# A gated recurrence inside a long one-core program: decay levels on column quarters of TensorE, and the value units read out of PSUM by ScalarE

## The chip, the cores and the metric

The program runs on one core of one Trainium2 chip. The metric is the device time of one execution in microseconds (us). A core has TensorE (PE in the profile, with its weight loads on a row of their own, PEld), VectorE (DVE), ScalarE (ACT), GpSimd (POOL) and SyncE (SP). Each runs its own queue of instructions in order, and they meet through semaphores. Matmul results land in PSUM, eight banks of 128 x 512 fp32 values; everything else lives in SBUF.

## The reference, cut to what matters

The program computes four layers of a model (each a feed-forward net, a mixer, a second feed-forward net and a gate) and then a second block, on 256 tokens of width 1024. Layers 0 and 3 use the mixer that the change touches, a gated recurrence with 8 heads of 128 features and chunks of 64 tokens:

```
def hgrn2_mixer(x, lb, w_in, g_norm, w_out):
    q, f, i, og = jnp.split(x @ w_in, 4, axis=-1)
    q = jax.nn.silu(q)
    log_f = jnp.logaddexp(jnp.log(lb), jnp.log1p(-lb) + jax.nn.log_sigmoid(f))
    k = (1.0 - lb) * jax.nn.sigmoid(-f)
    ...
    def step(S, inp):
        q_, k_, v_, g_ = inp
        b = jnp.cumsum(g_, axis=2)
        o_inter = jnp.einsum('bhtk,bhkv->bhtv', q_ * jnp.exp(b), S)
        diff = b[:, :, :, None, :] - b[:, :, None, :, :]
        decay = jnp.exp(jnp.where(causal[:, :, None], diff, -jnp.inf))
        A = jnp.einsum('bhtk,bhsk,bhtsk->bhts', q_, k_, decay)
        o_intra = jnp.einsum('bhts,bhsv->bhtv', A, v_)
        ...
    o = rmsnorm(from_chunks(o), g_norm)
    o = o.reshape(B, T, D_MODEL).astype(x.dtype) * jax.nn.silu(og)
    return o @ w_out
```

The values v are the columns `i` of the projection, one factor of the input norm per token.

## The kernel before

**Projections.** All weights arrive as units of 128 x 2048 fp32 values (1 MB), 405 of them in the order of use. ACT rounds a unit to the fp32r format (`high`, L1153: `w_hi`), DVE subtracts that from the unit (`low`, L1559: `w_lo`), and PE multiplies in three passes (high by high, low by high, high by low), so a unit is 48 matmuls of 256 columns: `project` (L670) with the weights stationary, `project_tokens` (L687) with the tokens stationary. There are three slots of split units. `high(m)` waits until unit m-3 has been used, `low(m)` waits for `high(m)`, and the projection of unit m waits for `low(m)`. So the end of unit u on PE releases `high(u+3)` on ACT, and that releases `low(u+3)` on DVE.

**The mixer's stages.** Units 0 to 3 give the forget gate, 4 to 7 the queries, 8 to 11 the values, 12 to 15 the output gate, 16 to 19 the output projection. A value unit is projected into one of two PSUM banks with the tokens on the partitions. `tokens(u)` evicts it into `HG_V`: two 128 x 256 operations with one factor per token (`rcol`), on DVE by `scale_tokens` (L1624). The last of the two raises `bank_read`, which counts evicted banks.

**The levels.** The matrix of decayed scores A of each head and block of 128 tokens is built from a diagonal (`diagonal`, L799) and seven levels l = 0 to 6 with windows w = 1, 2, 4, 8, 16, 32 and 64: at level l, the queries of the upper half of every window of 2w tokens meet the keys of the lower half of the same window. `level(l)` on PE (L819) runs over 16 groups of 128 tokens in two halves of eight. In levels 0 to 5 a group is two fp32 matmuls, one for each block of 64 tokens: 64 keys stationary, 32 queries moving, the result on partitions 0 to 63 or 64 to 127 of PSUM. Level 6 is one matmul a group. Each fp32 matmul leaves two records in the trace, each with a weight load of its own.

Between the levels DVE multiplies the decays of one more window into the queries and keys (`grow(l)`, L1826 and L1827, twice each, for the two halves). `grow(l)` waits for `level(l)`, since it overwrites its operands, and half of `level(l+1)` waits for the same half of `grow(l)`. For the levels 0 to 3 DVE copies the results that a mask picks out of PSUM into `HG_AT` (`take(l)`, L1842). For 4 to 6 ACT copies rectangles (L1276). `across` (L830) comes after level 6 in the same way.

**Order of the work.** It is written by hand. PE: unit 8, diagonal, level 0, unit 9, level 1, first half of unit 10, level 2, rest of unit 10, a quarter of unit 11, level 3, rest of unit 11, level 4, half of unit 12, level 5, rest of unit 12, a quarter of unit 13, level 6. DVE: evict 8, low 11, grow 0, diagonal, take 0, evict 9, low 12, grow 1, take 1, grow 2, evict 10, low 13, take 2, grow 3, take 3, evict 11, low 14, grow 4, grow 5, evict 12, low 15, grow 6. ACT in this stage has the `high` of units 11 to 14 and then the rectangles. Units from 12 on are evicted by `scale` (L1618) on DVE.

Of the kernel before, what the change touches and what calls it, by code (L numbers as in the profile page):

```python
# [11 lines left out]
ACT = mybir.ActivationFunctionType  # L12
AX_X = mybir.AxisListType.X

P = 128
T = 256
TB = T // P
# [16 lines left out]
HD = 64  # L34
# [186 lines left out]


LEVELS = (1, 2, 4, 8, 16, 32, 64)
MASKED = 4
NEG = -1e30

# [81 lines left out]
def build(nc, phases, x_t, p_t, mem_t, weights, smalls_d, post_rows, c_common, c_levels, c_swa, c_second, out):  # L308
    begin = starts(phases)
    NU = begin[-1]["units"]  # L310
    with ExitStack() as ctx:
# [235 lines left out]
        def level_bank(l):  # L547

            return 2 + (4 + 2 * l) % 6

        def upper(v, w):

            return v.rearrange("p (n a w) -> p n a w", a=2, w=w)[:, :, 1, :]
# [94 lines left out]
        def _(pe):  # L648
# [137 lines left out]
            def hg(i):  # L786
                m = own[i]
                n0, e0 = at(i, "units"), at(i, "banks")
                mixer_head(i)
                for u in range(4, 8):  # L790
                    project(n0 + u, e0 + u, XG)

                def diagonal():
                    pe.wait_ge(bank_read, e0 + 8 + 4)
                    pe.wait_ge(m["forget"], 4)
                    pe.wait_ge(m["qsilu"], 4)
                    for g in range(16):
                        h, b = g // 2, g % 2
                        last = nc.tensor.matmul(ps[:, 2 + g // 4, (g % 4) * P:(g % 4 + 1) * P],  # L799
                                                HG_K[:, h, b * P:(b + 1) * P], HG_Q[:, h, b * P:(b + 1) * P],  # L800
                                                start=True, stop=True)
                    last.then_inc(m["diag"], 1)

                def level(l):
                    w = LEVELS[l]
                    if l in (1, 2):
                        pe.wait_ge(m["masked"], 1)
                    elif 3 <= l <= 6:
                        pe.wait_ge(m["masked"], l - 1)
                    for half in range(2):  # L810
                        pe.wait_ge(m["qk"], 2 * l + half + 1)
                        for g in range(8):
                            at_ = (8 * half + g) * P
                            queries = P if w == HD else HD
                            for t in range(P // queries):
                                own_half = slice(at_ + t * HD, at_ + t * HD + queries)
                                c = g * HD + t * queries // 2
                                o = ps[t * HD:(t + 1) * HD, level_bank(l) + half, c:c + queries // 2]
                                last = nc.tensor.matmul(o.rearrange("p (n w) -> p n w", w=w),  # L819
                                                        HG_SUFFIX[:, own_half.start:own_half.start + HD],  # L820
                                                        upper(HG_PQ[:, own_half], w), start=True, stop=True)
                        last.then_inc(m["level"], 1)

                def across():
                    l = len(LEVELS)
                    pe.wait_ge(m["copied"], 1)
                    for half in range(2):
                        pe.wait_ge(m["qk"], 2 * l + half + 1)
                        for h in range(4 * half, 4 * half + 4):
                            last = nc.tensor.matmul(ps[:, level_bank(l) + half, (h % 4) * P:(h % 4 + 1) * P],  # L830
                                                    HG_SUFFIX[:, h * T:h * T + P], HG_PQ[:, h * T + P:(h + 1) * T],
                                                    start=True, stop=True)
                        last.then_inc(m["level"], 1)

                def outputs():
                    pe.wait_ge(bank_read, e0 + 12 + 4)
                    pe.wait_ge(m["masked"], 1 + MASKED)
                    pe.wait_ge(m["copied"], len(LEVELS) - MASKED + 1)
                    for h in range(HG_HEADS):
                        o = ps[:, 4 + h // 2, (h % 2) * T:(h % 2 + 1) * T]  # L840
                        v = HG_V[:, :, h * P:(h + 1) * P]
                        nc.tensor.matmul(o[:, 0:P], v[:, 0, :], HG_AT[:, 2 * h, :], start=True, stop=True)
                        nc.tensor.matmul(o[:, P:T], v[:, 0, :], HG_OFF[:, h, :], start=True, stop=False)
                        last = nc.tensor.matmul(o[:, P:T], v[:, 1, :], HG_AT[:, 2 * h + 1, :], start=False, stop=True)
                        if h % 2:
                            last.then_inc(m["o"], 1)

                def square_sums(p):
                    if p >= 2:
                        pe.wait_ge(m["logs"], p - 1)  # L850
                    pe.wait_ge(m["sq"], p + 1)
                    for c in range(2):
                        last = nc.tensor.matmul(ps[:, 2 + p % 2, c * T:(c + 1) * T], ones, HG_SQ[:, 2 * p + c, :],
                                                start=True, stop=True)
                    last.then_inc(m["sums"], 1)

                def both_sums(p):
                    square_sums(p)
                    square_sums(p + 1)
                project_tokens(n0 + 8, e0 + 8, XG, ring=2)  # L860
                diagonal()
                level(0)
                project_tokens(n0 + 9, e0 + 9, XG, ring=2)
                level(1)
                project_tokens(n0 + 10, e0 + 10, XG, ring=2, besides={4: lambda: level(2)})
                project_tokens(n0 + 11, e0 + 11, XG, ring=2, besides={2: lambda: level(3)})
                level(4)
                project(n0 + 12, e0 + 12, XG, ring=2, besides={4: lambda: level(5)})
                project(n0 + 13, e0 + 13, XG, ring=2, besides={2: lambda: level(6), 6: across})
                project(n0 + 14, e0 + 14, XG, ring=2, besides={2: outputs, 6: lambda: both_sums(0)})  # L870
                project(n0 + 15, e0 + 15, XG, ring=2, besides={0: lambda: both_sums(2)})
                pe.wait_ge(m["logs"], 4)
                pe.wait_ge(bank_read, e0 + 15 + 4)
                w_out(i, n0 + 16, e0 + 16)
# [270 lines left out]
        def _(act):  # L1145
            def high(m, dm=0, turn=0):

                if m >= NU:
                    return
                act.wait_ge(raw_full[m % RAW], 16 * turn + 16 * (m // RAW + 1))  # L1150
                if m >= SPLIT:
                    act.wait_ge(weights_used, m + 1 - SPLIT + dm)
                nc.scalar.copy(w_hi[:, m % SPLIT, :], raw[:, m % RAW, :]).then_inc(weights_hi, 1)  # L1153
# [92 lines left out]
            def hg(i):  # L1246
# [13 lines left out]
                for u in range(4, 8):  # L1260
                    high(n0 + u + SPLIT)
                    act.wait_ge(bank_read, e0 + u + 5)
                    q = HG_Q[:, 2 * (u - 4):2 * (u - 4) + 2]
                    nc.scalar.activation(q, q, ACT.Silu).then_inc(m["qsilu"], 1)
                for u in range(8, 12):
                    high(n0 + u + SPLIT)

                def copy_rectangles(l):
# [275 lines left out]
        def _(dve):  # L1544
# [75 lines left out]
            def scale_tokens(n, e, dst, col, ring=BANKS):  # L1620

                dve.wait_ge(weights_used, n + 1)
                for b in range(TB):
                    ins = V.tensor_scalar(dst[:, b], pair(e % ring, True)[:, b], rcol[:, col + b:col + b + 1], None,  # L1624
                                          ALU.mult)
                ins.then_inc(bank_read, 1)
# [157 lines left out]
            def hg(i):  # L1784
# [75 lines left out]
                    V.tensor_tensor(mo_lo[:, 2 * u:2 * u + 2], OUT[:, 2 * u:2 * u + 2],  # L1860
                                    mo_hi[:, 2 * u:2 * u + 2].bitcast(F32), ALU.subtract).then_inc(mo_ready, 1)

                def tokens(u):
                    scale_tokens(n0 + u, e0 + u, HG_V[:, :, 256 * (u - 8):256 * (u - 7)], 0, ring=2)

                def gate(u):
                    scale(n0 + 12 + u, e0 + 12 + u, HG_GATE[:, 2 * u:2 * u + 2], ring=2)
                for u in range(4, 8):
# [12 lines left out]
                    if u > 4:  # L1881
                        queries(u - 5)
                queries(3)
                tokens(8)
                low(n0 + 8 + SPLIT)
                grow(0)
                take_diagonal()
                take(0)
                tokens(9)
                low(n0 + 9 + SPLIT)  # L1890
                grow(1)
                take(1)
                grow(2)
                tokens(10)
                low(n0 + 10 + SPLIT)
                take(2)
                grow(3)
                take(3)
                tokens(11)
                low(n0 + 11 + SPLIT)  # L1900
                grow(4)
                grow(5)
                gate(0)
                low(n0 + 12 + SPLIT)
                grow(6)
# [438 lines left out]
```

## Time and profile before

| | us |
|---|---|
| median of 3 runs | 2610.75 |
| lowest and highest of them | 2608.72 and 2613.59 |
| the profiled execution, whole | 2613.3 |
| its span, first to last instruction | 2611.5 |
| mixer stage looked at, layer 0 | 261.35 to 297.43 in the span |
| the same stage, layer 3 | 1894.28 to 1930.36 in the span |

A line of the timeline gives start, duration, engine, source line, operation, what it writes and reads, its tile (partitions * columns of the stationary operand, then partitions x elements moved) and how many instructions were merged into it; a bracket gives the idle time of the engine before it and what ended that. Merged matmuls overlap, so the duration of a line of n is the time from the first start to the last end.

### The profile page before, as it was taken

How to read it: one execution, taken by the hardware profiler on the slowest of the kernel's cores; microseconds unless marked ns; L12 is line 12 of the kernel's file. 1: busy time of each engine (PE TensorE's matmuls, PEld its weight loads, DVE VectorE, ACT ScalarE, POOL GpSimd, SP SyncE). 2: the span in 40 equal slices, each digit the busy share in tenths (PEclk: the TensorE clock that was granted, in tenths of full speed). 3: DMA queues.
4: the chain of work that ended last, by engine and by line, in shares of the span. 5: the costliest groups of instructions: out<-in, count | busy, mean ns of one | idle time of the engine just before them, and what ended most of it. 6: DMA issues, size and time to landing. Idle time of an engine off the chain costs nothing.

```text
span 2611.5 us, 50243 instructions
## 1 busy us (share of the span) xinstructions
PE 2541.1 (97%) x21448; PEld 2497.3 (96%) x21448; DVE 1721.1 (66%) x2218; ACT 1197.1 (46%) x1272; POOL 29.3 (1%) x62
## 2 busy tenths in 40 slices
PE   8999999999999999999988999999999999999998
PEld 8999999999998999999977999999999999999998
DVE  6557676576565765775576656755766657788664
ACT  4345354354444543453464444533535434444643
POOL 0000000000000000000000000000000000011000
PEclk9999999999999999999988999999999999999999
DMA  7454345445544455545532554555434554444352
GB/s 272 178 182 174 113 147 197 177 178 182 186 166 144 150 185 186 177 178 183 184 135 69 179 191 167 189 179 179 176 114 159 199 178 175 165 138 167 137 188 74
DMA packets 61844, 437.12 MB, mean 167 GB/s; under 512 B 7472, under 2 KB 7600, under 8 KB 9456
## 3 DMA queue, kind: packets, MB, share of 16 engines
q1 hardware_dynamic: 59152, 426.95, 45.2%
q0 software_dynamic: 2528, 7.74, 1.0%
q8 instruction: 133, 2.18, 0.3%
q14 instruction: 31, 0.25, 0.0%
HBM read 430.47 MB, written 1.05 MB: 165 GB/s over the span
## 4 chain that ended last, share of the span: by engine, by line
PE 83%; DVE 11%; ACT 4%; issue 2%; DMA 0%; ACTq 0%; DVEq 0%
PE ps L670 53%; PE ps L701 19%; PE ps L687 5%; DVE w_lo L1559 3%; ACT w_hi L1153 2%; DVE scratch L1618 1%; DVE x L1677 1%; PE ps L819 1%; DVE right_lo L1612 1%; PE ps L943 1%; DVE right_hi L1609 1%; DVE left_lo L1612 1%; PE ps L966 0%; PE ps L952 0%; DVE left_hi L1609 0%
## 5 line engine op out<-in xcount | busy, mean ns | idle before, releaser
L1559 DVE TENSOR_TENSOR w_lo<-raw,w_hi 128x2048 fp32r<-128x2048 f32 x405 | 927.3, 2290 | 493.6 <-ACT w_hi L1153 493.3
L1153 ACT CAST w_hi<-raw 128x2048 fp32r<-128x2048 f32 x405 | 767.8, 1897 | 505.4 <-PE ps L701 249.2
L670 PE MATMUL ps<-right_hi,w_hi 128*128 128x256 f32 x2544 | 726.9, 286 | 7.1 <-DVE right_lo L1612 3.2
L670 PE MATMUL ps<-right_hi,w_lo 128*128 128x256 f32 x2544 | 720.3, 283 | 0.0
L670 PE MATMUL ps<-right_lo,w_hi 128*128 128x256 f32 x2544 | 720.2, 283 | 0.0
L670 PE MATMUL ps<-left_hi,w_hi 128*128 128x256 f32 x1968 | 563.8, 286 | 17.9 <-DVE left_lo L1612 15.1
L670 PE MATMUL ps<-left_hi,w_lo 128*128 128x256 f32 x1968 | 558.7, 284 | 0.0
L670 PE MATMUL ps<-left_lo,w_hi 128*128 128x256 f32 x1968 | 558.6, 284 | 0.0
L670 PEld LDWEIGHTS ps<-right_hi,w_hi 128*128 128x128 f32 x2544 | 488.6, 192 | 13.5 <-issue 5.1
L670 PEld LDWEIGHTS ps<-right_hi,w_lo 128*128 128x128 f32 x2544 | 488.7, 192 | 0.4
L670 PEld LDWEIGHTS ps<-right_lo,w_hi 128*128 128x128 f32 x2544 | 488.6, 192 | 0.0
L670 PEld LDWEIGHTS ps<-left_hi,w_hi 128*128 128x128 f32 x1968 | 379.6, 193 | 21.6 <-issue 14.4
L670 PEld LDWEIGHTS ps<-left_hi,w_lo 128*128 128x128 f32 x1968 | 379.7, 193 | 0.8 <-issue 0.5
L670 PEld LDWEIGHTS ps<-left_lo,w_hi 128*128 128x128 f32 x1968 | 379.6, 193 | 0.0
L1185 ACT ACTIVATE scratch<-scratch 128x256 f32<-128x256 f32 x176 | 73.7, 419 | 583.4 <-DVE scratch L1639 583.3
L701 PE MATMUL ps<-left_hi,w_hi 128*128 128x256 f32 x832 | 236.1, 284 | 2.9 <-DVE right_hi L1609 1.8
L701 PE MATMUL ps<-left_hi,w_lo 128*128 128x256 f32 x832 | 235.4, 283 | 0.0
L701 PE MATMUL ps<-left_lo,w_hi 128*128 128x256 f32 x832 | 235.4, 283 | 0.0
L701 PE MATMUL ps<-right_hi,w_hi 128*128 128x256 f32 x736 | 208.9, 284 | 1.8 <-DVE left_hi L1609 1.8
L701 PE MATMUL ps<-right_hi,w_lo 128*128 128x256 f32 x736 | 208.3, 283 | 0.0
L701 PE MATMUL ps<-right_lo,w_hi 128*128 128x256 f32 x736 | 208.3, 283 | 0.0
L1639 DVE TENSOR_TENSOR scratch<-ps,rstd 128x256 f32<-128x256 f32 x176 | 74.5, 423 | 156.4 <-PE ps L670 126.2
(290 smaller groups left out, 3079.0 us busy)
## 6 DMA issues: line engine op xcount, KB each, us to landing
raw<-weights_dram SPq DMA_DIRECT2D x405, 1024.0 KB, 4.8
scratch<-scratch POOLq DMA_DIRECT2D x48, 64.0 KB, 1.9
x<-x_t_dram SPq DMA_DIRECT2D x1, 1024.0 KB, 6.8
scratch<-c_second_dram POOLq DMA_DIRECT2D x1, 1024.0 KB, 7.8
scratch<-p_t_dram POOLq DMA_DIRECT2D x4, 256.0 KB, 3.0
scratch<-mem_t_dram POOLq DMA_DIRECT2D x1, 1024.0 KB, 8.3
out_dram<-scratch SPq DMA_DIRECT2D x2, 512.0 KB, 3.1
common<-c_common_dram POOLq DMA_DIRECT2D x1, 640.0 KB, 9.0
```

The source lines that it names most:

```text
L670: last = nc.tensor.matmul(bank(e, ring)[:, half * T:(half + 1) * T], l, r, start=(k == 0 and j == 0 and half == 0), stop=(k == KC - 1 and ...
L687: last = nc.tensor.matmul(bank(e, ring)[:, b * T:(b + 1) * T], l, r, start=(k == 0 and j == 0), stop=(k == KC - 1 and j == 2))
L701: last = nc.tensor.matmul(ps[:, 4 + c // 2, (c % 2) * T:(c % 2 + 1) * T], l, r, start=(first and k == 0 and j == 0 and c % 2 == 0), stop=( ...
L819: last = nc.tensor.matmul(o.rearrange("p (n w) -> p n w", w=w), HG_SUFFIX[:, own_half.start:own_half.start + HD], upper(HG_PQ[:, own_half] ...
L943: last = nc.tensor.matmul(ps[:, 3 + col // 512, col % 512:col % 512 + n], q, k, start=True, stop=True)
L1153: nc.scalar.copy(w_hi[:, m % SPLIT, :], raw[:, m % RAW, :]).then_inc(weights_hi, 1)
L1185: nc.scalar.activation(FFN_T[:, 2 + j % 2], FFN_T[:, j % 2], ACT.Silu).then_inc(silu_ready, 1)
L1559: V.tensor_tensor(w_lo[:, m % SPLIT, :], raw[:, m % RAW, :], w_hi[:, m % SPLIT, :].bitcast(F32), ALU.subtract).then_inc(weights_split, 1)
L1609: V.tensor_scalar(xg_hi[:, c], x[:, c], gain(g, c), None, ALU.mult).then_inc(x_updated, 1)
L1612: V.scalar_tensor_tensor(xg_lo[:, c], x[:, c], gain(g, c), xg_hi[:, c].bitcast(F32), ALU.mult, ALU.subtract).then_inc(xg_ready, 1)
L1618: V.tensor_tensor(dst, pair(e % ring, True), row(rstd[:], 2), ALU.mult).then_inc(bank_read, 1)
L1639: V.tensor_tensor(FFN_T[:, j % 2], pair(e)[:, 0], rstd[:], ALU.mult).then_inc(up_scaled, 1)
```

## The change

Two edits. In `level(l)` the tokens of a group are cut into parts of `max(32, 2w)` instead of 64, so in levels 0 to 4 a group is four matmuls, each with 32 keys stationary, 16 queries moving, and its result on one of four quarters of 32 partitions in PSUM. Levels 5 and 6 stay as they are. And `tokens(u)` moves from DVE to ACT: two activations (Copy, with the factor per token as scale) right in front of `high(u+3)` in ACT's queue, for the four value units. DVE gets one new wait, on those evictions, before its first eviction of a gate unit.

```diff
--- before.py
+++ after.py
@@ -221,6 +221,7 @@
 
 
 LEVELS = (1, 2, 4, 8, 16, 32, 64)
+QUARTER = 32
 MASKED = 4
 NEG = -1e30
 
@@ -811,14 +812,14 @@
                         pe.wait_ge(m["qk"], 2 * l + half + 1)
                         for g in range(8):
                             at_ = (8 * half + g) * P
-                            queries = P if w == HD else HD
-                            for t in range(P // queries):
-                                own_half = slice(at_ + t * HD, at_ + t * HD + queries)
-                                c = g * HD + t * queries // 2
-                                o = ps[t * HD:(t + 1) * HD, level_bank(l) + half, c:c + queries // 2]
+                            part = max(QUARTER, 2 * w)
+                            keys = min(part, HD)
+                            for t in range(0, P, part):
+                                c = g * HD + t // 2
+                                o = ps[t:t + keys, level_bank(l) + half, c:c + part // 2]
                                 last = nc.tensor.matmul(o.rearrange("p (n w) -> p n w", w=w),
-                                                        HG_SUFFIX[:, own_half.start:own_half.start + HD],
-                                                        upper(HG_PQ[:, own_half], w), start=True, stop=True)
+                                                        HG_SUFFIX[:, at_ + t:at_ + t + keys],
+                                                        upper(HG_PQ[:, at_ + t:at_ + t + part], w), start=True, stop=True)
                         last.then_inc(m["level"], 1)
 
                 def across():
@@ -1262,7 +1263,16 @@
                     act.wait_ge(bank_read, e0 + u + 5)
                     q = HG_Q[:, 2 * (u - 4):2 * (u - 4) + 2]
                     nc.scalar.activation(q, q, ACT.Silu).then_inc(m["qsilu"], 1)
+
+                def tokens(u):
+                    act.wait_ge(bank_read, e0 + u + 4)
+                    act.wait_ge(weights_used, n0 + u + 1)
+                    for b in range(TB):
+                        ins = nc.scalar.activation(HG_V[:, b, 256 * (u - 8):256 * (u - 7)], ps[:, (e0 + u) % 2, b * T:(b + 1) * T],
+                                                   ACT.Copy, scale=rcol[:, b:b + 1])
+                    ins.then_inc(bank_read, 1)
                 for u in range(8, 12):
+                    tokens(u)
                     high(n0 + u + SPLIT)
 
                 def copy_rectangles(l):
@@ -1860,9 +1870,6 @@
                     V.tensor_tensor(mo_lo[:, 2 * u:2 * u + 2], OUT[:, 2 * u:2 * u + 2],
                                     mo_hi[:, 2 * u:2 * u + 2].bitcast(F32), ALU.subtract).then_inc(mo_ready, 1)
 
-                def tokens(u):
-                    scale_tokens(n0 + u, e0 + u, HG_V[:, :, 256 * (u - 8):256 * (u - 7)], 0, ring=2)
-
                 def gate(u):
                     scale(n0 + 12 + u, e0 + 12 + u, HG_GATE[:, 2 * u:2 * u + 2], ring=2)
                 for u in range(4, 8):
@@ -1881,25 +1888,22 @@
                     if u > 4:
                         queries(u - 5)
                 queries(3)
-                tokens(8)
                 low(n0 + 8 + SPLIT)
                 grow(0)
                 take_diagonal()
                 take(0)
-                tokens(9)
                 low(n0 + 9 + SPLIT)
                 grow(1)
                 take(1)
                 grow(2)
-                tokens(10)
                 low(n0 + 10 + SPLIT)
                 take(2)
                 grow(3)
                 take(3)
-                tokens(11)
                 low(n0 + 11 + SPLIT)
                 grow(4)
                 grow(5)
+                dve.wait_ge(bank_read, e0 + 12 + 4)
                 gate(0)
                 low(n0 + 12 + SPLIT)
                 grow(6)
```

## Rows read from the trace of the kernel before

**Rows 1.** The page: PE's busy line, and the chain that ended last by engine.

```profile
PE 2541.1 (97%) x21448; PEld 2497.3 (96%) x21448; DVE 1721.1 (66%) x2218; ACT 1197.1 (46%) x1272; POOL 29.3 (1%) x62
...
PE 83%; DVE 11%; ACT 4%; issue 2%; DMA 0%; ACTq 0%; DVEq 0%
```

**Rows 2.** Timeline of PE in layer 0: levels, ends of units 9 and 11.

```profile
264.86 2.06 PE L819 MATMUL ps<-scratch 128*64 128x32 f32 x64
...
272.58 0.28 PE L687 MATMUL ps<-w_hi,left_lo 128*128 128x256 f32 x1
272.79 2.06 PE L819 MATMUL ps<-scratch 128*64 128x32 f32 x64
...
278.53 2.24 PE L819 MATMUL ps<-scratch 128*64 128x32 f32 x64 [0.61 <-DVE scratch L1827]
...
291.49 0.28 PE L687 MATMUL ps<-w_hi,left_lo 128*128 128x256 f32 x1
291.69 2.06 PE L819 MATMUL ps<-scratch 128*64 128x32 f32 x64
...
297.43 2.24 PE L819 MATMUL ps<-scratch 128*64 128x32 f32 x64 [0.61 <-DVE scratch L1827]
...
304.10 2.08 PE L819 MATMUL ps<-scratch 128*64 128x64 f32 x32
```

**Rows 3.** Busy time in short stretches inside levels 3 and 6, L819 alone.

```profile
285.42:285.45 0.04, 0.04 (x8) 0.04 (x6) 1.00 0.00 0
...
304.30:304.34 0.04, 0.04 (x4) 0.04 (x3) 1.00 0.00 0
```

**Rows 4.** Weight loads and matmuls of other widths: timeline, then durations (ns, min/median/max).

```profile
225.53 0.60 PE L729 MATMUL ps<-common,rstd 1*128 1x1 f32 x4
...
L819 PEld LDWEIGHTS ps<-scratch x832: 132/138/138, 264.9 to 1938.8; 128*64 128x64 f32 x167
...
L882 PEld LDWEIGHTS ps<-x,tiny x16: 109/113/113, 799.1 to 802.2; 128*36 128x36 f32 x16
```

**Rows 5.** Timeline of DVE in the same stretch.

```profile
261.39 0.88 DVE L1624 TENSOR_SCALAR scratch<-ps,rcol 128x256 f32<-128x256 f32 x2 [0.27 <-PE ps L687]
...
274.88 2.29 DVE L1559 TENSOR_TENSOR w_lo<-raw,w_hi 128x2048 fp32r<-128x2048 f32 x1 [0.92 <-ACT w_hi L1153]
...
277.69 0.69 DVE L1827 TENSOR_TENSOR scratch<-scratch 128x512 f32<-128x512 f32 x1
...
285.87 2.29 DVE L1559 TENSOR_TENSOR w_lo<-raw,w_hi 128x2048 fp32r<-128x2048 f32 x1 [0.79 <-ACT w_hi L1153]
...
289.82 0.68 DVE L1827 TENSOR_TENSOR scratch<-scratch 128x512 f32<-128x512 f32 x1
...
293.79 2.29 DVE L1559 TENSOR_TENSOR w_lo<-raw,w_hi 128x2048 fp32r<-128x2048 f32 x1
...
296.60 0.69 DVE L1827 TENSOR_TENSOR scratch<-scratch 128x512 f32<-128x512 f32 x1
```

**Rows 6.** Timeline of ACT in the same stretch.

```profile
272.95 1.90 ACT L1153 CAST w_hi<-raw 128x2048 fp32r<-128x2048 f32 x1 [9.60 <-PE ps L687]
...
283.93 1.91 ACT L1153 CAST w_hi<-raw 128x2048 fp32r<-128x2048 f32 x1 [9.08 <-PE ps L687]
```

**Rows 7.** Timeline of ACT elsewhere: pairs of 128 x 256 activations ahead of a `high`.

```profile
2492.17 0.91 ACT L1512 ACTIVATE scratch<-scratch,smalls 128x256 f32<-128x256 f32 x2 [3.05 <-DVE scratch L1618]
2492.99 1.89 ACT L1153 CAST w_hi<-raw 128x2048 fp32r<-128x2048 f32 x1
...
2583.51 0.39 ACT L1527 ACTIVATE scratch<-ps 128x256 f32<-128x256 f32 x1 [4.36 <-PE ps L687]
...
2584.24 1.90 ACT L1153 CAST w_hi<-raw 128x2048 fp32r<-128x2048 f32 x1
```

**Rows 8.** Busy time of the stage in layer 0 and in layer 3.

```profile
261.35:297.43 36.08, 34.85 (x521) 33.68 (x520) 32.63 (x36) 9.06 (x8) 0.00 (x0) 1.00 0.32 118
1894.28:1930.36 36.08, 34.85 (x521) 33.68 (x520) 32.63 (x36) 9.06 (x8) 0.00 (x0) 1.00 0.32 118
```

The columns of the stretches in Rows 3 and 8 are: the stretch, its length, busy time and number of instructions of PE and PEld (in Rows 8 then of DVE, ACT and POOL), the granted TensorE clock, the share of the DMA engines, GB/s.

## The prediction, made before the changed kernel was run

> **What bounds the kernel now.** I read the page first. PE is busy for 97% of the span, and the chain that ended last is PE for 83% of it, DVE 11%, ACT 4% [rows 1]. On the whole, then, time taken off PE is time off the end. But the change touches two stages of 36 us, and there the average says little: in the stretch from the end of unit 8 to level 5, PE is busy for 34.85 of 36.08 us and DVE for 32.63, ACT for only 9.06 [rows 8]. Two engines are nearly full. So the second view is the timeline of PE [rows 2]: levels 2 and 5 begin after 0.61 us of idle time that a `grow` on DVE ended; the others begin without a wait. Third, the timelines of DVE and ACT [rows 5, 6]: of the four `low` of this stage three begin after DVE sat idle for `high` on ACT (0.92 and 0.79 us in two of these rows, the first has a like wait), and ACT had itself waited 9 us for PE to finish the unit. So the loop that sets the pace is: end of unit u on PE, `high(u+3)` 1.90, `low(u+3)` 2.2, first half of a `grow` 1.2, next level. Layer 3 repeats the stage to the hundredth [rows 8], so I work out layer 0 and count it twice.
>
> **Part 1, levels 0 to 4 on quarters.** Removed per level: 32 fp32 matmuls (64 records); added: 64 (128 records), with half the keys and half the queries each. What does a record cost? 64 records have their first and last start 2.06 - 0.22 = 1.84 us apart, 29 ns each; level 6 has twice the moving columns and 32 records in 2.08, 60 ns each [rows 2]. The moving columns do not explain it: four records with a single moving column and 128 columns of weights start (0.60 - 0.25)/3 = 117 ns apart [rows 4]. The load of the weights does: about 58 ns for 64 columns, 112 for 128. And two halves of the array load and multiply side by side: inside a level with alternating halves eight matmuls are in flight at a time, in level 6, which uses one half only, four [rows 3]. So today a pair of records takes 58 ns. A load of 36 columns lasts 113 ns against 138 for 64 [rows 4], 25 ns less for 28 columns; for 32 columns I get 58 - 29 = about 30 ns. If the four quarters overlap as the two halves do, four records take 30 to 32 ns, and a level is 32 x 31 = 1.0 us instead of 1.84. That is 0.84 us for a level, 4.2 for a mixer, 8.4 for the kernel, all on PE. No row shows four quarters; the bounds are 0.9 us a level (28 ns for four) and, if only two overlap, 64 x 31 = 2.0 us. I take 1.0, since both the width of the load and the overlap of column groups are seen.
>
> **Part 2, the eviction on ACT.** DVE loses four times 0.84 to 0.88 us per mixer [rows 5]. ACT gains two activations of 128 x 256 ahead of `high`. Nearest rows: from the start of such a pair out of PSUM to the start of the `high` behind it 0.73 us (with two reads of an accumulator between), and 0.82 for a pair out of SBUF [rows 7]. I take 0.78; bounds 0.56 (the pair of L1527 without the reads) and 0.85. ACT is idle three quarters of the stage, but both the eviction and `high` wait for the same event, the end of the unit, so the 0.78 is not hidden: it stands in the loop above, where DVE was already waiting for ACT. What is queued behind it: `high(u+3)`, hence `low(u+3)`, hence `grow`, hence the next level. The time that DVE saves mostly turns into a longer wait for `high`. DVE's new wait before the first gate unit costs nothing: unit 11 was evicted some 10 us earlier. The next use of the bank by PE is a whole unit later.
>
> The Trainium skill (ScalarE: Activation LUTs, "Table sets: the hidden batching unit") counts copy among the functions in every table set, so no table load would be added; no row here shows a Copy activation with a scale. Were one added, the idle ACT would take it before the unit ends, and the sum would be the same.
>
> **The sum, layer 0.** Level 0 ends 0.84 earlier, so unit 9 ends at 272.58 + 0.28 - 0.84 = 272.02. ACT evicts from 272.1, `high(12)` runs 272.9 to 274.8; it ended at 272.95 + 1.90 = 274.85 before [rows 6]. DVE, which had waited 0.92 us for it [rows 5], still waits. `low(12)` starts at 274.8 (274.88), the first half of `grow(1)` ends at about 278.3 instead of 277.69 + 0.69 = 278.38 [rows 5]. So level 2 begins at 278.45 instead of 278.53: of 1.68 us gained by PE 0.08 arrives, and PE waits 2.2 us in front of level 2. Level 2's first half takes 0.5, its second waits for the second half of `grow(1)` (1.2 after the first) and takes 0.5: its last start is at 280.05 instead of 280.54, gain 0.5. Unit 10 ends 0.5 earlier; ACT had started there at 283.93 [rows 6] and now finishes `high(13)` at 283.43 + 0.78 + 1.9 = 286.1 against 285.84: DVE is now 0.25 late. The first half of `grow(3)` ends at 289.82 + 0.68 + 0.25 = 290.75. Meanwhile PE has gained 0.5 + 0.84 = 1.34, ends unit 11 at 290.43 and stands before level 4 at 291.69 - 1.34 = 290.35: it waits till 290.8, and again between the halves, and leaves the level 1.05 ahead of before. ACT evicts unit 11 from 290.5, `high(14)` ends at 293.2, `low(14)` starts there instead of at 293.79 [rows 5], 0.6 earlier, and level 5 at 297.43 - 0.58 = 296.85. PE, 1.05 ahead, waits for it. Level 5 and all behind it hang on that start: the `scale` of the gate units, `high(15)` and `grow(6)` wait for ends on PE. So 0.58 us a mixer, 1.15 for the kernel.
>
> The profiled execution took 2613.3, so this gives 2612.1. It lay 2.55 above the median; taken from the median the forecast is 2610.75 - 1.15 = **2609.6 us**. With 28 ns and an eviction of 0.56 the same steps give 1.26 a mixer (2608.2), with a level of 1.2 us and 0.85 they give a loss of 0.1 (2611.0).
>
> **The rivals.** *A: the levels get no shorter.* Two of the four quarters overlap, or something else keeps a level at 1.84 to 2.0 us. For it: no row has four column groups. Against it: rows 3. Then the loop is longer by the eviction and PE gives nothing back. `high(12)` ends 0.75 late by the eviction ahead of it, and level 2 starts as late; unit 10, `high(14)` and level 5 get the delay of level 2 and one more eviction on top, since PE never waits elsewhere: level 5 starts 1.5 (levels as now) to 2.0 late (2.0 us a level). Kernel +3.0 to +4.0: 2613.8 to 2614.8.
>
> *B: the rate of instructions, slower.* The change doubles the matmuls and the weight loads of five levels. If PE cannot start records faster than today's mean of 29 ns [rows 2], a level takes 127 x 29 = 3.7 us, 1.85 more. From 15 ns a record upward a level costs more than now, and from about 18 the loss passes 5 us. Levels 0 to 4 then cost 9.2 us more per mixer; the waits before levels 2 and 5 (0.61 us each) absorb part: some 8 us a mixer, 16 in all, 2627. Half way, at 22 ns, a level is 2.8 us, the mixer 4.3 longer, 2619.4. For it: nothing in the trace runs faster than 29 ns on the mean. Against it: 29 ns is just what the weight load of two halves explains.
> The Trainium skill (TensorE: Matmul & The Clock Gate, "Wait — 56ns, not 53.3ns?") says that matmuls never start less than about 25 ns apart, however few columns they move. The mean of 29 ns here does not refute it. By that rule, as an estimate, a level is 3.2 us and the kernel 2621.5, inside B.
>
> *C: more than forecast.* A gain of over 5 us needs 2.6 a mixer, where the loop through ACT and DVE yields at most about 1.3. Only an eviction that costs the loop nothing and levels that free DVE too would do it.
>
> **How the numbers follow.** Forecast 0.57, A 0.20, B 0.17, C 0.06. The medians of this kernel spread by about 0.1% each way, and 0.2% (5.2 us) is about what a measurement of it can tell from no change. The forecast and A lie within it: same 0.77; B is slower, 0.17; C faster, 0.06. The range takes in the forecast's bounds and A, each with 1.6 us of spread: 2606.6 to 2616.0; B and C are left out.
>
> **What would show it.** In the changed profile: L819 records of 128*32 with 16 moving, 128 to a level, a level's line at about 1.2 us in levels 0, 1 and 3 (1.8 in 2 and 4, with the wait between halves); PE idle some 2.2 us before level 2, 1.1 before level 5 and half a microsecond before level 4, ended by L1827; DVE idle before each `low` longer than 0.9, ended by ACT; two activations of 128 x 256 and about 0.38 each before `high` 11 to 14. Lines of L819 at 2.1 us mean A, above 3 B. The forecast is wrong if level 5 starts more than a microsecond from 296.85.

## The result: slower, and the profile after

The changed kernel takes 2617.11 us (median of 12 runs, 2613.81 to 2619.49) against 2609.91 for the kernel before, measured beside it (12 runs, 2607.16 to 2613.59). The ratio is 1.0027, with a 95% interval of 1.0019 to 1.0035: 0.27% or 7.2 us slower. The forecast was 2609.6 and within 0.2%. It was wrong, and its range (up to 2616.0) ended 1 us below the measured time.

The page of the changed kernel shows next to nothing: PE 97%, the chain 82% PE instead of 83%. Only the number of its instructions has grown (21448 to 22088 matmul records). The span went from 2611.5 to 2617.7 us.

```profile
PE 2539.4 (97%) x22088; PEld 2495.5 (95%) x22088; DVE 1714.7 (66%) x2202; ACT 1203.2 (46%) x1288; POOL 29.4 (1%) x62
...
PE 82%; DVE 11%; ACT 4%; issue 2%; DMA 0%; ACTq 0%; DVEq 0%
```

The stage tells more. All that follows is in terms of one length, the **stretch** from the first matmul of level 0 to the first of level 5. Before, it was 297.43 - 264.86 = 32.57 us in layer 0 [rows 2] and the same in layer 3. Now it is 301.56 - 264.63 = 36.93 us, and 1936.92 - 1900.22 = 36.70 in layer 3: 8.5 us in the two. The timeline of PE in the changed kernel, to be read beside rows 2 (L820 is the line of the levels now, L688 that of the value units, L671 that of the gate units):

```profile
264.63 1.30 PE L820 MATMUL ps<-scratch 128*32 128x16 f32 x128
...
265.86 0.38 PE L688 MATMUL ps<-w_hi,left_hi 128*128 128x256 f32 x1
266.28 0.38 PE L688 MATMUL ps<-w_lo,left_hi 128*128 128x256 f32 x1
...
272.10 1.29 PE L820 MATMUL ps<-scratch 128*32 128x16 f32 x128
...
278.57 0.73 PE L820 MATMUL ps<-scratch 128*32 128x16 f32 x64 [2.11 <-DVE scratch L1837]
279.68 0.79 PE L820 MATMUL ps<-scratch 128*32 128x16 f32 x64 [0.39 <-DVE scratch L1837]
...
280.79 0.41 PE L688 MATMUL ps<-w_lo,left_hi 128*128 128x256 f32 x1
281.00 0.41 PE L688 MATMUL ps<-w_hi,left_lo 128*128 128x256 f32 x1
...
292.50 0.72 PE L820 MATMUL ps<-scratch 128*32 128x16 f32 x64 [0.38 <-DVE scratch L1837]
293.61 0.59 PE L820 MATMUL ps<-scratch 128*32 128x16 f32 x46 [0.39 <-DVE scratch L1837]
296.70 0.36 PE L820 MATMUL ps<-scratch 128*32 128x16 f32 x18 [2.50 <-issue]
...
297.57 0.42 PE L671 MATMUL ps<-left_hi,w_hi 128*128 128x256 f32 x1
...
301.56 2.06 PE L820 MATMUL ps<-scratch 128*64 128x32 f32 x64
```

Three things are to be seen. *The levels are short*, 1.29 us a line instead of 2.06, and PE waits before level 2 and inside levels 2 and 4 for DVE, as forecast; the wait before level 5 that was forecast is not there. *Behind level 2 the matmuls of the value unit start 0.21 us apart* (280.79, 281.00) where they start 0.12 apart elsewhere. *And in the middle of level 4 PE stops* for 2.5 us, and what ended it is neither another engine nor a DMA of data but "issue". Behind this stop too the matmuls are slow. The stretches by clock (the number behind the bracketed counts of the last engine is the granted TensorE clock):

```profile
278.00:280.40 2.40, 1.44 (x128) 1.34 (x128) 2.40 (x4) 0.00 (x0) 0.00 (x0) 0.96 0.88 253
280.40:283.60 3.20, 3.20 (x19) 3.20 (x16) 3.20 (x4) 0.00 (x0) 0.00 (x0) 0.50 0.35 143
...
294.10:296.70 2.60, 0.10 (x12) 0.00 (x1) 2.48 (x2) 0.74 (x1) 0.00 (x0) 1.00 0.10 38
296.70:300.70 4.00, 4.00 (x36) 3.97 (x37) 2.88 (x5) 1.45 (x4) 0.00 (x0) 0.57 0.54 176
```

So the clock is at 0.50, the lower of its two levels (1.2 instead of 2.4 GHz), right behind the long wait of level 2 and behind the stop of level 4. In the kernel before it was 1.00 in the whole stage [rows 8]; in the changed one the mean over either mixer's stage is 0.92. ACT shows the eviction where it was expected, with the split behind it:

```profile
272.27 0.84 ACT L1271 ACTIVATE scratch<-ps,rcol 128x256 f32<-128x256 f32 x2 [8.41 <-PE ps L688]
273.00 1.90 ACT L1154 CAST w_hi<-raw 128x2048 fp32r<-128x2048 f32 x1
```

### The profile page after: what moved, and what is told of

Its sections match the earlier page's. It is cut to its first block, busy times and chain, and to the rows that moved or that the text cites. A ratio compares the mean times of both kernels' runs of the same rounds, so it can differ in the third digit from the quotient of the medians.

```text
span 2617.7 us, 51533 instructions
## 1 busy us (share of the span) xinstructions
PE 2539.4 (97%) x22088; PEld 2495.5 (95%) x22088; DVE 1714.7 (66%) x2202; ACT 1203.2 (46%) x1288; POOL 29.4 (1%) x62
## 4 chain that ended last, share of the span: by engine, by line
PE 82%; DVE 11%; ACT 4%; issue 2%; DMA 0%; ACTq 0%; DVEq 0%
PE ps L671 54%; PE ps L702 19%; PE ps L688 5%; DVE w_lo L1569 3%; ACT w_hi L1154 2%; DVE scratch L1628 1%; DVE x L1687 1%; DVE right_lo L1622 1%; PE ps L944 1%; DVE right_hi L1619 1%; DVE left_lo L1622 1%; PE ps L967 0%; PE ps L953 0%; DVE left_hi L1619 0%; DVE x L1703 0%
## 5 line engine op out<-in xcount | busy, mean ns | idle before, releaser
L671 PE MATMUL ps<-right_hi,w_hi 128*128 128x256 f32 x2544 | 727.6, 286 | 7.2 <-DVE right_lo L1622 3.2
L671 PE MATMUL ps<-right_hi,w_lo 128*128 128x256 f32 x2544 | 721.0, 283 | 0.0
L671 PE MATMUL ps<-right_lo,w_hi 128*128 128x256 f32 x2544 | 720.8, 283 | 0.0
L671 PE MATMUL ps<-left_hi,w_hi 128*128 128x256 f32 x1968 | 564.1, 287 | 18.1 <-DVE left_lo L1622 15.4
L671 PE MATMUL ps<-left_hi,w_lo 128*128 128x256 f32 x1968 | 559.2, 284 | 0.0
L671 PE MATMUL ps<-left_lo,w_hi 128*128 128x256 f32 x1968 | 559.0, 284 | 0.0
L671 PEld LDWEIGHTS ps<-right_hi,w_hi 128*128 128x128 f32 x2544 | 489.2, 192 | 13.6 <-issue 5.0
L671 PEld LDWEIGHTS ps<-right_hi,w_lo 128*128 128x128 f32 x2544 | 489.4, 192 | 0.4
L671 PEld LDWEIGHTS ps<-right_lo,w_hi 128*128 128x128 f32 x2544 | 489.3, 192 | 0.0
L671 PEld LDWEIGHTS ps<-left_hi,w_hi 128*128 128x128 f32 x1968 | 380.0, 193 | 21.8 <-issue 14.7
L671 PEld LDWEIGHTS ps<-left_hi,w_lo 128*128 128x128 f32 x1968 | 380.1, 193 | 0.7 <-issue 0.2
L671 PEld LDWEIGHTS ps<-left_lo,w_hi 128*128 128x128 f32 x1968 | 380.0, 193 | 0.0
```

The lines of the kernel that those rows point to most:

```text
L671: last = nc.tensor.matmul(bank(e, ring)[:, half * T:(half + 1) * T], l, r, start=(k == 0 and j == 0 and half == 0), stop=(k == KC - 1 and ...
```

## The experiments

The theory from these rows: the forecast's mechanism is right, but the short levels bring on two things that it did not have, **a halved clock** behind a long wait and **a stop for instructions** behind a dense burst. The rival: the eviction in front of the split, part of the loop, is what lengthens the stage. Diffs are against the changed kernel. The stretch is given for layer 0 and layer 3. Times of the kernel are ratios to the kernel before, run beside it. From execution to execution the time between the two mixers, where the kernels do the same work, moves by some us (from level 5 of layer 0 to level 0 of layer 3: 1600.4 us in the profile of before, 1598.7 changed, 1600.5 and 1594.8 in two of the kernels below), so differences under 2 us are read from the stretch and not from the medians.

### Quarters alone

```diff
                 for u in range(8, 12):
-                    tokens(u)
                     high(n0 + u + SPLIT)
```

and `tokens(u)` back in its four places on DVE (cut to what matters).

> Quarters in levels 0 to 4, evictions left on DVE. Theory (half clock and fetch pause, both brought on by the short bursts): a level still takes about 1.1 us, level 4 still stops for some 2.7 us, and the stretch from level 0 to level 5 is 34 to 36 us against 32.57 before and 36.93 changed; the kernel is 3 to 6 us slower than before. Rival (the eviction on ACT in front of the split is what lengthens the stage): the stretch is 31.2 us, 1.4 us shorter than before, and the kernel 2.8 us faster.

Measured: stretch 34.27 and 33.60 us, ratio 1.0009 (1.0000 to 1.0019). PE waits 1.66 us before level 2, no half clock follows, but level 4 stops in both mixers and the clock behind it is halved:

```profile
290.46 1.42 PE L820 MATMUL ps<-scratch 128*32 128x16 f32 x110
294.38 0.36 PE L820 MATMUL ps<-scratch 128*32 128x16 f32 x18 [2.50 <-issue]
...
291.80:294.30 2.50, 0.08 (x8) 0.00 (x0) 2.50 (x4) 0.72 (x1) 0.00 (x0) 1.00 0.07 23
294.60:298.00 3.40, 3.40 (x29) 3.37 (x18) 3.18 (x5) 1.45 (x4) 0.00 (x0) 0.51 0.32 101
```

The rival's 31.2 us is out: with no eviction on ACT the quarters still lose 1.0 to 1.7 us a mixer. The theory's 34 to 36 was a little high, since one of its two half clocks is missing.

### The eviction alone

```diff
-                            part = max(QUARTER, 2 * w)
-                            keys = min(part, HD)
-                            for t in range(0, P, part):
+                            queries = P if w == HD else HD
+                            for t in range(P // queries):
```

and the rest of the loop of the levels as in the kernel before (cut).

> Evictions on ACT, all levels in halves as before. Theory: bursts of 1.84 us, no pause within a level, PE idle about 1.4 us before level 2, full clock throughout; the stretch is 32.57 + 1.5 = 34.1 us, the kernel about 3 us slower than before, and no more. Rival (the eviction alone makes the loss): the stretch is 36 us or more and the kernel 7 us slower.

Measured: stretch 34.04 and 34.04 us, where 34.1 was worked out; ratio 1.0003 (0.9993 to 1.0012), less than the 3 us expected of the medians. No stop, no half clock, though PE waits 1.6 us before levels 2 and 5. So the eviction in front of the split costs 1.47 us a mixer, through the loop, and nothing else.

```profile
278.24 2.24 PE L820 MATMUL ps<-scratch 128*64 128x32 f32 x64 [1.35 <-DVE scratch L1837]
```

### Fillers in the waits

A filler is a matmul put where PE would wait, into a bank that the level then overwrites: eight before level 2, one before level 4.

```diff
+                    for _ in range({2: 8, 4: 1}.get(l, 0)):
+                        nc.tensor.matmul(ps[:, level_bank(l), 0:P], ones, ident, start=True, stop=True)
                     for half in range(2):
                         pe.wait_ge(m["qk"], 2 * l + half + 1)
```

> The change, with eight filler matmuls (1.8 us of PE) in front of level 2 and one in front of level 4, into the bank that the level then overwrites. Theory: the stretch behind level 2 keeps the full clock and unit 10 ends some 1.5 us earlier than in the changed kernel; if the fetch pause in level 4 goes or moves is open, since the fillers shift the instructions by 36. Stretch 33 to 35.5 us, kernel 2 to 5 us faster than the changed one. Rival (the clock falls because of the small matmuls themselves, not the idle time): the half clock behind level 2 stays.

Measured: stretch 33.62 and 34.09 us, ratio 1.0014 (1.0004 to 1.0024). The half clock behind level 2 is gone in both mixers, with the small matmuls of levels 0 to 2 as in the changed kernel. So it came of the idle time and not of the small matmuls alone. And it came back where this kernel has a wait of 2.17 us, before level 5 (the last line below):

```profile
275.68 1.95 PE L812 MATMUL ps<-common 128*128 128x128 f32 x16
277.86 0.74 PE L822 MATMUL ps<-scratch 128*32 128x16 f32 x64 [0.23 <-DVE scratch L1839]
...
280.00:283.40 3.40, 3.40 (x30) 3.40 (x30) 3.40 (x5) 0.44 (x2) 0.00 (x0) 1.00 0.28 116
295.50:297.50 2.00, 0.18 (x2) 0.00 (x0) 2.00 (x4) 0.00 (x0) 0.00 (x0) 1.00 0.27 33
299.20:302.60 3.40, 3.40 (x33) 3.34 (x30) 2.12 (x4) 1.16 (x2) 0.00 (x0) 0.50 0.38 159
```

The stop in level 4 is gone as well; instead there is one of 1.2 us (layer 0) and 1.4 us (layer 3) between two starts in the middle of unit 11, behind level 3. The half clock behind level 5 lies outside the stretch, which ends there. From level 5 to level 6 this kernel takes 8.14 and 9.57 us where the changed one takes 6.50 and 6.49, so the stretch flatters it: part of the loss has moved, and the kernel is still slower than before.

### Level 4 in halves

```diff
-                            part = max(QUARTER, 2 * w)
+                            part = max(QUARTER if l < 4 else HD, 2 * w)
```

> The change with level 4 left in halves (levels 0 to 3 on quarters). Theory (the fetch of instructions cannot follow 256 instructions in 1.1 us): level 4 has 128 instructions in 1.84 us and does not stop; without the pause the clock behind it stays full too; the stretch is 36.93 - 2.7 - 1.4 + 0.3 = about 33.1 to 34 us, the half clock behind level 2 stays. Kernel 5 to 7 us faster than the changed one, within 1 us of before. Rival (the pause comes from something else at that time, such as the weights or the wait): it stays near level 4 at 2.7 us.

Measured: stretch 34.18 and 36.24 us, ratio 1.0012 (1.0002 to 1.0021), 3 us over the kernel before where 1 us was expected. In layer 0 it is as expected but for 0.2 us: no stop in level 4, the half clock behind level 2 only. In layer 3 the stop is there, but behind level 2, among plain matmuls of unit 10. So it belongs neither to level 4 nor to the line of the levels. The half clock comes behind this stop; behind the wait of 2.39 us before level 2 it did not come in this mixer, and the granted clock is 1.00 from 1913.20 to 1919.70:

```profile
1915.91 0.28 PE L688 MATMUL ps<-w_lo,right_hi 128*128 128x256 f32 x1
1918.57 0.39 PE L688 MATMUL ps<-w_hi,right_lo 128*128 128x256 f32 x1 [2.38 <-issue]
```

What is under way in these stops? The DMA queues of the stop here (1915.95 to 1918.50) and of the one in the changed kernel (294.00 to 296.70) each list one packet of instructions; in the first 0.4 us of the latter (294.05 to 294.45) there is none yet. By the times of the packets in the traces, each of 16 KB, this is the same in all seven stops of 2.6 to 2.9 us of the kernels here: the packet begins 0.4 to 0.5 us after the last start on PE. In the four stops of 1.1 to 1.4 us in unit 11 it ends within about 0.1 us of where the stop begins. And in all eleven PE goes on 1.2 to 1.5 us after the end of the packet. That fits a PE that has run out of instructions and waits for the next block. The trace does not say for which engine a packet is, or when it was asked for, so this much is inferred.

```profile
q1 hardware_dynamic: 26, 0.08, 7.9%
q8 instruction: 1, 0.02, 2.3%
```

### As many instructions, slowly

The eviction alone, with each matmul of levels 0 to 4 issued twice (the second overwrites the first with the same values). The diff is against the kernel with the eviction alone:

```diff
-                                last = nc.tensor.matmul(o.rearrange("p (n w) -> p n w", w=w),
+                                for _ in range(2 if l < 5 else 1):
+                                    last = nc.tensor.matmul(o.rearrange("p (n w) -> p n w", w=w),
```

> Evictions on ACT, levels 0 to 4 in halves with each matmul issued twice: 256 instructions a level as in the change, but in 3.7 us instead of 1.1. If the stops come from the rate at which instructions are used up, there is none over 0.5 us in this kernel and no half clock; the stretch is 34.04 + 5 x 1.85 less the idle time = about 40 to 41 us. If they come from the number or the place of the instructions, one of 2.7 us a mixer stays and the stretch is 43 us or more.

Measured: stretch 40.46 and 40.46 us, ratio 1.0048 (1.0032 to 1.0063). No matmul of the two stretches starts over 0.33 us after the one before it, and PE is busy for the whole of it at full clock:

```profile
263.54 3.95 PE L821 MATMUL ps<-scratch 128*64 128x32 f32 x128
...
263.54:304.00 40.46, 40.46 (x809) 39.59 (x808) 29.33 (x29) 9.33 (x13) 0.00 (x0) 1.00 0.25 82
```

A level has as many instructions as in the change, in 3.7 us instead of 1.1. So the stops come with the rate at which instructions are used up, not with their number.

### Both causes out, the eviction in

Level 4 in halves as above, and eight fillers before level 2.

> The change with eight fillers before level 2 and level 4 in halves; the evictions stay in front of the splits. It takes away both the half clock behind level 2 and the stop in level 4, and leaves what the forecast summed up. If its sum was right but for these two, the stretch is 32.0 to 33.0 us in a mixer without a stop and the clock is full. If the sum was wrong elsewhere, the stretch is over 34 us with neither.

Measured: full clock in both mixers; stretch 32.13 us in layer 3, where nothing stops, and 33.53 in layer 0, with a stop of 1.1 us in unit 11 and one of 0.4 in unit 9. Ratio 1.0003 (0.9994 to 1.0012). The forecast's own sum was 296.85 - 264.86 = 31.99 us. It holds to 0.14 us in the mixer where its two omissions are taken away. Level 4 in halves costs PE 0.73 us there, and it does not show, since PE still waits before level 5 (1.01 us between two starts).

### The eviction behind the split

```diff
-                    tokens(u)
                     high(n0 + u + SPLIT)
+                    tokens(u)
```

> The change with each eviction on ACT behind the split of the next unit instead of in front of it. If the eviction stands in the loop at 0.75 us, PE's idle time before level 2 falls from 2.4 to about 1.6 us, as with the evictions on DVE, and no half clock follows level 2; the stop inside level 4 stays, since its 256 instructions are the same, and brings the half clock behind it. Stretch from level 0 to level 5: 33.5 to 34.5 us against 36.93. If the eviction's place does not matter, the stretch stays at 36.9.

Measured: stretch 34.27 and 35.37 us, ratio 1.0009 (0.9999 to 1.0018), so the place matters. In layer 3 that is 0.9 us over the range expected. The wait before level 2 fell to 1.66 us as expected, but the half clock behind level 2 was there in both mixers, against the expectation:

```profile
276.40:278.00 1.60, 0.27 (x3) 0.06 (x1) 1.60 (x4) 0.00 (x0) 0.00 (x0) 1.00 0.09 10
280.30:283.60 3.30, 3.30 (x18) 3.30 (x17) 3.30 (x5) 0.00 (x0) 0.00 (x0) 0.50 0.23 92
```

With the same wait of 1.66 us the quarters alone kept the full clock, so behind a wait of this length the outcome is not a matter of the wait alone. In layer 0 there is also a stop of 2.69 us in level 4 behind which the clock stayed at 1.00, and that makes most of the difference between the two mixers.

The same order with all levels in halves (`part = max(HD, 2 * w)`):

> Only the evictions moved, behind the splits, all levels in halves. If the loop through ACT and DVE is what sets the pace, DVE's saved 0.86 us per eviction turns into waiting for ACT: the stretch is 32.5 to 32.6 us, as before, against 34.04 with the evictions in front, and the kernel within 1 us of before. If DVE's load itself sets the pace, it is 30 to 31 us.

Measured: stretch 32.56 and 32.57 us, ratio 1.0004 (0.9994 to 1.0013). DVE is rid of 3.4 us a mixer, and nothing comes of it: from the end of unit 8 to level 5 in layer 0 its waits for the splits on ACT are 6.2 us instead of 2.8.

### A version that beats both

Evictions behind the splits, eight fillers before level 2, level 4 in halves:

> Evictions behind the split, eight fillers before level 2, level 4 in halves: all three causes treated. If they are all there is, the stretch is 31.5 to 32.3 us against 32.57 before, without a half clock, and the kernel 0.5 to 2 us faster than before. If a stop for instructions comes up elsewhere (it moved to unit 10 in one mixer with level 4 in halves), that mixer is 2.5 to 4 us longer and the kernel no faster than before.

Measured: ratio 0.9987 (0.9978 to 0.9996), 2607.22 us against 2609.87. Stretch 30.66 us in layer 3, 32.62 in layer 0, both at full clock; the difference is again stops behind bursts, 1.4 us between two starts in unit 11 and 0.7 in unit 9. Both branches of the expectation were missed: the mixer without a stop is 0.8 us shorter than its range, and the kernel is faster although the other mixer has a stop. By the stretches the whole gain, 1.9 us, comes from layer 3.

```profile
1893.83:1924.49 30.66, 30.00 (x762) 29.06 (x761) 28.10 (x28) 9.26 (x13) 0.00 (x0) 1.00 0.32 108
263.55:296.17 32.62, 30.54 (x762) 29.19 (x761) 28.05 (x28) 9.25 (x13) 0.00 (x0) 1.00 0.30 101
...
286.29 0.39 PE L688 MATMUL ps<-w_hi,left_hi 128*128 128x256 f32 x1 [1.11 <-issue]
```

With level 3 in halves too (`QUARTER if l < 3`):

> As the kernel with evictions behind the splits, eight fillers before level 2 and level 4 in halves, but level 3 in halves too. The stop behind level 3 (1.39 us in one mixer there) should go, and 0.73 us of level 3 is given back: stretch 31.2 to 31.8 us in a mixer without a stop against 30.66, no half clock, kernel 1 to 2 us faster than before. If the stops come from a fixed place in the code and not from the burst just before them, one stays behind level 3.

Measured: stretch 31.74 and 31.89 us, ratio 1.0001 (0.9992 to 1.0011). As expected the stop behind level 3 goes with the burst of level 3, and what is left is one of 0.4 to 0.5 us behind level 0. The gain of 1 to 2 us that was expected of the kernel does not show in the ratio.

With levels 0 and 1 on quarters and no fillers (`QUARTER if l < 2`), the evictions still behind the splits:

> Evictions behind the splits, only levels 0 and 1 on quarters, no fillers. PE idle before level 2 about 1.6 us, as in the two kernels with that wait, so a half clock behind it in some of the mixers (it was there in two of four); stop of 0.4 to 0.7 us behind level 0 at most. Stretch 31.8 to 32.3 us without a half clock, 33.2 with one; kernel within 1.5 us of before.

Measured: stretch 32.11 and 33.30 us, ratio 1.0004 (0.9995 to 1.0014). The wait before level 2 is 1.67 us in both, and the half clock followed in one of them, which makes the difference.

## Why the prediction was wrong, by its own steps

**Part 1 held.** Four quarters overlap: 128 records start within 1.29 - 0.18 = 1.11 us, 8.7 ns each on the mean, 35 ns for four where 30 to 32 were forecast, and a level is 1.11 us instead of 1.0. In a stretch of 0.03 us inside level 3, 26 matmuls are under way where eight were [rows 3], and the load of 32 columns lasts 109 ns, as read off rows 4:

```profile
L820 PEld LDWEIGHTS ps<-scratch x1472: 106/109/158, 264.6 to 1945.2; 128*32 128x32 f32 x160, 128*64 128x64 f32 x24
...
286.90:286.93 0.03, 0.03 (x26) 0.03 (x17) 1.00 0.00 0
```

Rival A is out by this. So is the 25 ns between the starts of matmuls that the Trainium skill gives as a floor (TensorE: Matmul & The Clock Gate, "Wait — 56ns, not 53.3ns?"): the mean here is 8.7 ns.

**Part 2 held.** The eviction takes 0.73 us from its start to that of the split, forecast 0.78; alone it costs 1.47 us a mixer, as the prediction reckoned for levels that get no shorter (1.5), and behind the split nothing. No table load came with it: the program has 79 of them before and after.

**The sum held as far as it went**, and its wait before level 2 too: 2.11 us idle before level 2 at 278.57 (2.2 at 278.45 forecast). Two small slips in it change nothing here. The last start of level 2 is 280.15 by its own terms (278.45 + 1.2 + 0.5) and not 280.05, and the top of the range is 2614.8 + 1.6 = 2616.4 and not 2616.0; the measured 2617.11 is above both.

**What failed is a step that was priced at nothing: "PE waits 2.2 us in front of level 2".** The wait itself was free, since DVE set the start of level 2 anyway. But behind it the clock was halved, and the next 15 starts of unit 10 came 0.213 us apart instead of 0.120: 1.4 us, behind which everything hangs on PE. The second failure is the treatment of the rate of instructions. Rival B had the right place and the wrong form: it looked for a floor on the time between starts, found none below 29 ns in the trace, and made it 4.3 to 8 us a mixer. In fact PE starts records at 8.7 ns on the mean, and then, in the burst or up to several us behind it, stops for 0.4 to 2.9 us until a packet of instructions has come. The prediction had no term for such a stop.

In numbers, layer 0 against the forecast's 31.99 us: level 2 starts 0.35 late relative to level 0 (278.57 - 264.63 = 13.94 against 13.59; there is a gap of 0.42 between two starts at the head of unit 9). Level 4 starts 1.93 late (27.87 against 25.94): the 0.35, 1.4 of half clock and 0.2 more. From level 4 to level 5 it is 9.06 us instead of 6.05: 2.7 between two starts for the stop, 1.5 of half clock behind it (16 starts), less the 1.1 us that PE would have waited before level 5 anyway. Together 4.9, the measured 36.93. Level 5 starts at 301.56, 4.7 us from the 296.85 of the forecast, which called itself wrong from one microsecond on. Halved clock and stops are thus about equal parts. Two mixers give 8.5 us more than before; the span shows 6.2 and the medians 7.2, within what the rest of the program moves from one execution to the next.

Why did nothing in the forecast lead there? Rows 8 gave a clock of 1.00 and were read for the busy time only. The waits before levels 2 and 5 were 0.61 us [rows 2], and a wait more than three times as long was put into the sum without asking what it does to the clock. The same page of the Trainium skill ("HAM oscillation — how this bites in real kernels") warns that idle gaps between bursts of matmuls throttle PE again. The runs agree with it in kind, since fillers in the same gap kept the clock at 1.00. The waits of its example, for DMA, are about 3 to 5 us; here the clock fell behind waits of 2.1 to 2.4.

What stays open: what decides behind a given wait. The half clock followed three of six waits of 1.66 us before level 2 of kernels with quarters, and five of six waits of 2.1 to 2.4 us. It followed none of six waits of 1.62 to 1.63 us (four in the kernel with halves, two before level 5 of the kernels with level 4 in halves). Nor was it tried whether other places of the same instructions in the program would avoid the stops; their place and length differed between the two mixers of one kernel.

## What to carry to other kernels

When an edit makes one engine faster than what feeds it, the gain turns into waiting, and on TensorE waiting is not free: ask of every wait that a sum leaves or lengthens what the clock does behind it (here it fell behind half of the waits of 1.66 us and nearly all of 2.1 us and more), and fill it if need be. Many small instructions in a short time have a second price that the mean time per instruction of a slower version does not show: look behind each burst for idle time ended by "issue". And work that moves to an idle engine goes behind, not in front of, what that engine does for the critical loop: here the order of two lines was 1.5 us a mixer.

## What the runs showed of the hardware

- Four column quarters of the array load and multiply side by side: 128 records of 32 columns of weights and 16 moving in 1.11 us. On halves, 64 records take 1.84 us.
- The clock went to 0.50 behind five of six PE waits of 2.1 to 2.4 us before a level (counted between two starts: 2.39 and 2.14 in the changed kernel, 2.17 twice in the one with fillers, 2.39 twice in the one with level 4 in halves, where it fell in layer 0 only), behind three of six waits of 1.66 us, and behind six of seven stops of 2.6 to 2.9 us. As a rule some 15 matmuls then started 0.21 us apart instead of 0.12, which is about 1.4 us. Behind level 5 of layer 3 in the kernel with fillers it lasted twice as long (1930.78 to 1937.61).
- In kernels with bursts of 256 instructions in 1.1 us PE stopped for 0.4 to 2.9 us between two starts, in the burst or behind it, and went on 1.2 to 1.6 us after a packet of instructions of 16 KB had ended. 256 instructions in 3.7 us brought no such stop.
